# The last round of a two-table expert gather, requested table by table instead of group by group

## The reference, cut to what matters

```python
# peer_ffn: each token picks 8 heads x 16 = 128 experts of 16384; u_tab and v_tab are (16384, 2048)
h = gelu(einsum('td,thkd->thk', xc, u_tab[ic]))          # 128 dot products per token
out = einsum('thk,thkd->td', gc * h, v_tab[ic])          # weighted sum of 128 rows per token
x = x + out
gate = sigmoid(rmsnorm(x, w) @ ple_w_gate)               # 2048 x 2048
x = x + gate * (p @ ple_w_proj)
```

## Time and profile before

| what | value |
|---|---|
| median of 3 runs | 2944.87 us (2942.80 to 2945.95) |
| profiled execution, whole time | 2945.74 us |
| its span in the trace | 2943.9 us |
| outside of the span (the difference) | 1.84 us |
| PE / DVE / ACT / POOL busy share of the span | 91% / 59% / 28% / 23% |
| DMA queue of the row requests (q0) | 536.90 MB |
| chain that ended last, largest parts | PE 62%, DMA 24% |

### The profile page before, as it was taken

How to read it: one execution, slowest core, us unless ns; L and a number is a source line. 1 busy time by engine, 2 the same in 40 slices (tenths; PEclk the granted TensorE clock), 3 DMA queues, 4 the chain that set the end, 5 groups by cost and what they waited for, 6 DMA issues and landing times.

```text
span 2943.9 us, 29068 instructions
## 1 busy us (share of the span) xinstructions
PE 2668.0 (91%) x11107; PEld 1842.1 (63%) x11107; DVE 1744.8 (59%) x2610; ACT 836.7 (28%) x1215; POOL 691.8 (23%) x647
## 2 busy tenths in 40 slices
PE   9999999999999999999999777877777887787789
PEld 8888888888888888887896333333333333333347
DVE  5666556654566555555677888655545555555555
ACT  5545544433344444435542000000000100000023
POOL 0000000000000000000006655655444554545510
PEclk9999999999999999999999988999999999999999
DMA  7555556555565555652459999999999999999984
GB/s 262 165 169 171 172 178 193 187 187 199 186 186 186 193 192 183 219 162 86 158 167 386 421 422 422 422 422 422 422 417 419 421 422 422 422 422 422 422 337 143
DMA packets 275349, 839.60 MB, mean 285 GB/s; under 512 B 16263, under 2 KB 114291, under 8 KB 209188
## 3 DMA queue, kind: packets, MB, share of 16 engines
q0 software_dynamic: 73728, 536.90, 43.9%
q1 hardware_dynamic: 200284, 298.44, 30.7%
q10 hardware_dynamic: 1224, 2.70, 0.3%
HBM read 835.86 MB, written 2.13 MB: 285 GB/s over the span
## 4 chain that ended last, share of the span: by engine, by line
PE 62%; DMA 24%; DVE 5%; POOL 5%; issue 3%; ACT 1%; POOLq 0%; DVEq 0%; SPq 0%; ACTq 0%
DMA vrows<-in_peer_u,idxc 24%; PE bank L1855 11%; PE bank L2303 8%; PE bank L1810 8%; PE bank L1813 8%; PE bank L1812 8%; PE bank L1857 6%; DVE vrows L1648 2%; POOL vrows L2427 2%; POOL idxc L2418 2%; PE bank L1832 2%; PE bank L1836 2%; PE bank L1834 2%; PE bank L2236 1%; PE bank L2238 1%
## 5 line engine op out<-in xcount | busy, mean ns | idle before, releaser
L1009 DVE TENSOR_TENSOR wl<-raw,wh 128x1024 fp32r<-128x1024 f32 x544 | 652.0, 1209 | 580.7 <-ACT wh L580 577.9
L580 ACT CAST wh<-raw 128x1024 fp32r<-128x1024 f32 x544 | 558.5, 1037 | 667.8 <-PE bank L1813 338.9
L1855 PE MATMUL bank<-AhAl,wh 128*128 128x512 f32 x1408 | 498.7, 399 | 0.3 <-DVE wl L1009 0.3
L1648 DVE CUSTOM_DVE_ANT_0 big<-big,tmp 128x2048 f32<-128x2048 f32 x128 | 293.1, 2292 | 223.0 <-DMA big<-in_peer_u,idxc 222.1
L1648 DVE CUSTOM_DVE_ANT_0 vrows<-vrows,tmp 128x2048 f32<-128x2048 f32 x128 | 292.9, 2292 | 214.4 <-DMA vrows<-in_peer_u,idxc 213.3
L1857 PE MATMUL bank<-AhAl,wl 128*128 128x256 f32 x1408 | 395.4, 281 | 0.0
L867 ACT ACTIVATE hgel<-hcur,rstd 128x2 f32<-128x2 f32 x128 | 37.7, 295 | 1177.4 <-DVE hcur L1648 1177.4
L2303 PE MATMUL bank<-big,gbc 128*128 128x512 f32 x512 | 249.8, 645 | 69.0 <-DVE gbc L1665 69.0
L2303 PE MATMUL bank<-vrows,eacc 128*128 128x512 f32 x512 | 250.7, 648 | 67.2 <-DVE eacc L1665 67.1
L1855 PEld LDWEIGHTS bank<-AhAl,wh 128*128 128x128 f32 x1408 | 264.6, 188 | 66.0 <-issue 0.6
L2303 PE MATMUL bank<-vrows,gbc 128*128 128x512 f32 x512 | 246.8, 640 | 60.8 <-DVE gbc L1665 57.7
(11 more groups left out here) (340 smaller groups left out, 3927.1 us busy)
## 6 DMA issues: line engine op xcount, KB each, us to landing
raw<-in_mlp_w SPq DMA_DIRECT2D x128, 1024.0 KB, 5.2
raw<-in_sb_w_qkv SPq DMA_DIRECT2D x48, 1024.0 KB, 5.2
raw<-in_w_in SPq DMA_DIRECT2D x28, 1024.0 KB, 4.9
raw<-in_sb_w_o SPq DMA_DIRECT2D x16, 1024.0 KB, 5.0
raw<-in_w_out SPq DMA_DIRECT2D x16, 1024.0 KB, 5.1
raw<-in_peer_w_q SPq DMA_DIRECT2D x16, 1024.0 KB, 5.0
raw<-in_ple_w_gate SPq DMA_DIRECT2D x16, 1024.0 KB, 5.1
big<-line SPq DMA_DIRECT2D x4, 768.0 KB, 7.4
```

The lines of the kernel that those rows point to most:

```text
L580: nc.scalar.copy(whv[hq % 4][:, :, 0:width], raw_half[hq][:, :, 0:width]).then_inc(hi_done, 1)
L1009: V_.tensor_tensor(wlv[hq % 4][:, :, 0:width], raw_half[hq][:, :, 0:width], whf[hq % 4][:, :, 0:width], ALU.subtract).then_inc(split_done, 1)
L1648: V_.tensor_tensor_reduce(out=ubuf[g][b], in0=ubuf[g][b], in1=xn[:, m, :], scale=1.0, scalar=0.0, op0=ALU.mult, op1=ALU.add, accum_out=hcu ...
L1855: nc.tensor.matmul(o[:, :].rearrange("p (x s) -> p x s", x=2), whw[s][:, c, bs_], Ahl[:, :, kc, :], start=kc == 0, stop=False, skip_group_ ...
```

## The change

POOL's hardware loop for the second half of tile 1 stops one round earlier. The last round is written out: first the eight `peer_u` requests of all groups, each behind its own dot of the round before (a wait for `dots_done[g]`), then the eight `peer_v` requests, each behind its own sum of the round before (`v_done[g]`). The expert numbers are read from `idx` directly, so the last round has no index copies. No other engine's program is changed: the dots, weights and sums keep their order.

```diff
-            with pool.Fori(per // 2, per) as i:
+            with pool.Fori(per // 2, per - 1) as i:
                 more_rows(1, i)
+
+            def last_row(table, dst, g, b, landed_):
+
+                s = SLOTS + (per - 1) * GROUPS * EG + g * EG + b
+                nc.gpsimd.indirect_dma_start(
+                    out=dst, out_offset=None, in_=table,
+                    in_offset=bass.IndirectOffsetOnAxis(ap=idx[:, s:s + 1], axis=0),
+                ).then_inc(landed_, 16)
+
+            for g in range(GROUPS):
+                for b in range(EG):
+                    pool.wait_ge(dots_done[g], EG * (2 * per - 2) + b + 1)
+                    last_row(a["peer_u"], ubuf[g][b], g, b, u_landed[g][b])
+            for g in range(GROUPS):
+                for b in range(EG):
+                    pool.wait_ge(v_done[g], EG * (2 * per - 2) + EG + b + 1)
+                    last_row(a["peer_v"], vbuf[g][b], g, b, v_landed[g][b])
```

## The result

| kernel | median of its runs | span of the profiled execution |
|---|---|---|
| before | 2944.4 us (2942.02 to 2947.72, 13 runs) | 2943.9 us |
| changed | 2950.73 us (2949.77 to 2952.56, 13 runs) | 2948.2 us |

The ratio of the changed kernel to the one before, in runs side by side, is 1.0022 with a 95% interval of 1.0015 to 1.0029: about 6 us slower. The profiled execution of the changed kernel took 2950.06 us.

What follows compares the result with a forecast made beforehand. DMA bounds the gather, PE the tail behind it. First `peer_v` row 2825.6 + sums 27.7 + clock 2.8 = 2856.1 against 2850.16, so +5.9 on the median 2944.87: 2950.8 us, range 2945.5 to 2953.5.

Steps and rivals of the forecast that it cites:

- No gain in the gather, requests far ahead: Row gather: DMA engines are never free, so no request order shortens it if requests queue ahead; 2.487 us a row.
- Index copies: 0: POOL's four index copies and their waits: covered, since a request stands 24 us ahead of its landing; worth 0.
- Dots early, off the chain: DVE in the last round: dots through at 2829.3, every diagonal ready before its `peer_v` row.
- PE's sums in one piece: 27.7 us: PE in the last round: all eight rows' sums stand behind 2825.6 and take 27.7 us at full clock.
- The clock: 2.8 us: PE at the start of the last round's sums: half clock adds 2.8 us, with bounds of 1.7 to 3.05.
- The gate loads: 0: SP's gate weight loads: start 2.7 us earlier, first split not later, four blocks on hand when sums end; worth 0.
- Rival B: PE waits for rows inside the sums as gate loads share the DMA engines: +8.9 us, 2953.8 us; chance 0.12.
- the start of these sums is always on the half level: PE's last-round sums: half clock is the default, released by sustained activity, so they start on it; 2.8 us.
- queues taking turns packet by packet: DMA engines under gate loads: the rows' 8 KB packets lose little to the loads' smaller ones; adds nothing.
- Rival A: PE starts the last sums earlier or runs them at full clock: 2948.0, 2943.8 or 2941.0 us; chance 0.17.
- C: POOL reaches the new requests too late, or the queue keeps group order: no change, 2944.9 us; chance 0.06.
- the sums waited about equally for dots and rows: Last sums before the change: diagonals ready at 2841.41, last two `peer_v` rows landing at 2840.5 and 2843.0.

Runs made afterwards that it cites:

- half sums: Last round's sums cut to two of four banks for seven of eight rows: in the changed kernel 2944.39 us, in the kernel before 2943.19 us.
- the changed kernel again: The changed kernel run once more without edits, as partner on the same chip: 2950.18 us, ratio 1.0017 to the kernel before.
- with loads held: Changed kernel with SP's first gate load held until the second table's last row has landed: 2951.05 us, ratio 1.0021 to the kernel before.
- two groups ahead: Changed kernel with its last-round requests in the order u0 u1 u2 v0 u3 v1 v2 v3: 2946.55 us, ratio 1.0006 to the kernel before.
- 19 matmuls: Changed kernel with 19 matmuls into unused banks on PE ahead of the last round's sums: 2948.44 us, ratio 1.0013 to the kernel before.
- the two middle orders: Changed kernel with first-table requests one group ahead of the second table's, or two: 2945.28 and 2946.55 us, ratios 1.0003 and 1.0006.
- the last version: Kernel before, with PE's last-round gaps filled by matmuls and group 3's gelu and diagonals made slot by slot: 2943.39 us, ratio 0.9995.

## Why the prediction was right

The forecast was 2950.8 us, the changed kernel's median is 2950.73, and it was slower by the ratio 1.0022, at the line of 0.2% between *within* and *slower*. The mechanism was right; that the two times agree to 0.1 us is luck, since the change was 6.3 us where 5.9 was forecast, and the clock alone moves an execution by 1.4. Point by point:

- **No gain in the gather, requests far ahead.** Right. The first row of the second table in the changed kernel is taken up 2825.26 − 2805.38 = 19.9 us behind the first dot, which is 8 × 2.487.
- **Index copies: 0.** Right: 44.49 us with the copies gone and the order kept. POOL's new waits cost nothing either: the first row of the second table lands where the pace puts it.
- **Dots early, off the chain.** Right. Last diagonal forecast 23.6 us behind the first dot; it is at 2828.2, 22.8 us behind. That they would gain next to nothing even without PE behind them rests on an estimate from the traces with half sums.
- **PE's sums in one piece: 27.7 us.** Right: 27.7 us from 2826.68 to 2854.42 where the clock stayed up, 29.2 us in the changed kernel, where it did not.
- **The clock: 2.8 us.** Near on the mean, not for each execution. The profiled one lost 1.5 us, two others like it 2.9 (the changed kernel again, and with loads held), 2.5 on the mean. So its last round is 4.6 us longer than before's, others' 6.1; the median moved by 6.3. The choice of 2.8 had luck in it: it was taken from the sum behind "the longest gap, 5.73 us", but the trace of the kernel before has two longer ones, of 5.81 us (16 instructions in 8.80 us, so 1.7 over) and of 5.82 (32 in 17.13, so 3.2 over). These would have given anything from 1.7 to 3.2. The gap itself was 16.8 us and not 13.8, as round 14's last sums ran at full clock this time:

```profile
1695.04 8.80 PE L2303 MATMUL bank<-vrows,eacc 128*128 128x512 f32 x16 [5.81 <-DVE eacc L1665]
...
1856.60 17.13 PE L2303 MATMUL bank<-vrows,eacc 128*128 128x512 f32 x32 [5.82 <-DVE eacc L1665]
```

- **The gate loads: 0.** Right for the sum, but its reason was too weak. Rival B's mechanism exists: the loads stretch the last rows from 2.49 to 3.27 us each. The prediction argued against it from 3 packets in 1 us in both cases, which is too short a stretch to tell 3.2 from 2.5 packets (by 8 packets of 8 KB for each engine and row, 8 / 2.487 and 8 / 3.27). It decides nothing here: PE wants the last row 3.43 us before its end, 45.7 us behind the first dot, and with half sums and loads beside them PE found it landed at 39.7. The 8.5 us that B's paragraph gives to the rows still on the way should be 7.7 by its own start of the loads, 2835.3; nothing hangs on it.
- **The Trainium skill's rules.** "TensorE: Matmul & The Clock Gate", Part 1: the rule taken from it, that the start of these sums is always on the half level, agrees with all seven profiles of the changed order or of two groups ahead in which PE had been idle for 4.8 us or more (1.5 to 2.9 us lost), and with the pair with and without 19 matmuls. "DMA: Bandwidth & Descriptors", Queues, rings and completion order: queues taking turns packet by packet was taken to mean that rows lose little; they lose 0.8 us in 2.5. By one 2 KB packet of the loads for each 8 KB packet of the rows, 2.49 us would become 3.11 (an estimate by bytes), which is near the 3.27; but a packet in that section is a batch of several descriptors, so whether these are the same packets no run here shows.

Rival A (no clock loss, or rows that land sooner) is ruled out by the traces, C by POOL's rows. What the runs cannot settle is the size of the two middle orders' loss by time alone; it rests on their traces.

One thing the prediction had only in half: it said that the sums waited about equally for dots and rows before the change. The half sums and the last version show a third event within 1.2 us of the copy, the split of the first gate weights. With the gate loads where they are, even a change that had brought the sums forward could have gained no more than that.

## What to carry to other kernels

When the last stage of a streamed pipeline is slower for each item than the stream (3.43 us against 2.49 here), its items must be spread over the stream; putting them all last exposes the difference times their number, plus whatever its idle time before costs in clock. Before moving work off the end of a chain, add up what the next engine would have in front of it from its first input on, and look for the event that comes within a microsecond of the one removed. And compare two profiles by distances between events of the same stage, since their absolute times differ by more than such an edit is worth.

## What the runs showed of the hardware

- The clock's loss at the start of the sums, after 16.8 us of idle, was 1.5 us in one execution and 2.9 in two; it was 2.3 us after 11.90 us of idle (two groups ahead), 2.8 after 4.84 and nothing after 0.54. The length of the gap does not set it: in the kernel before, gaps of 5.7 to 5.8 us were followed by 1.7, 2.8 and 3.2 us.
- Loads on another DMA queue slow the rows by about a third: 1 MB rows that landed 2.49 us apart landed 3.24 to 3.29 us apart while weight loads of 1 MB ran beside them, and again 2.45 and 2.48 apart when these were held.
- A weight load that starts 3.7 us sooner need not land sooner: in the changed kernel SP starts at 2834.02 and DVE's first split at 2846.42, which is 28.6 and 41.0 us behind the first dot; before it is 2838.00 and 2846.73, 32.3 and 41.1 us behind.
